# Hybrid decoder layer with mixture of experts: router logits from rows ahead of the layer norm, and second biases moved between weight chunks

## The reference

```python
xp = layer_norm(DN_ALPHA * xp + mix, ln1_g, ln1_b)
# moe_ffn
logits = (xf @ w_router + b_router).astype(F32)
top_v, top_i = lax.top_k(logits, TOP_K)          # 4 of 32
gates = jax.nn.softmax(top_v, axis=-1)
...
h = xb @ w1[e] + b1[e]
x_glu = jnp.minimum(h[:, 0::2], 7.0)
x_lin = jnp.clip(h[:, 1::2], -7.0, 7.0)
a = x_glu * jax.nn.sigmoid(1.702 * x_glu) * (x_lin + 1.0)
y = (a @ w2[e] + b2[e]) * gate
```

## Time and profile before

| | |
|---|---|
| median of 3 runs | 1467.37 us (1466.77 to 1469.71) |
| profiled execution | 1468.95 us, its span 1467.1 us |
| PE busy | 1334.4 us (91%) |
| DVE, ACT, POOL busy | 425.5, 336.8, 310.8 us |
| read from DRAM | 446.92 MB, 320 GB/s over the span |
| mean granted clock of TensorE | 0.957 |

### The profile page before, as it was taken

One profiled execution on the slowest core, in us unless ns is written; L12 is line 12 of the kernel. 1 busy time (PEld: TensorE's weight loads), 2 busy tenths in 40 slices (PEclk: granted clock), 3 DMA queues, 4 the chain that ended last, 5 costly groups with the idle time before them and its releaser, 6 DMA issues.

```text
span 1467.1 us, 32494 instructions
## 1 busy us (share of the span) xinstructions
PE 1334.4 (91%) x12921; PEld 636.8 (43%) x12921; DVE 425.5 (29%) x1085; ACT 336.8 (23%) x797; POOL 310.8 (21%) x322
## 2 busy tenths in 40 slices
PE   7999997899999999989999987899998799999871
PEld 6478765745433343433334332443433333343320
DVE  2141556656651122211112211211212121121313
ACT  1103313610022132222213122122312222131212
POOL 5215001113522221121212111122111112211103
PEclk9999997799599999999999999999999999999996
DMA  9265115070699999999999999999999999999943
GB/s 300 63 119 96 59 58 212 1 316 30 219 353 400 406 384 412 406 408 411 406 412 403 412 406 408 412 401 403 393 413 409 410 410 406 406 396 409 412 189 125
DMA packets 102821, 465.59 MB, mean 317 GB/s; under 512 B 31474, under 2 KB 41982, under 8 KB 53504
## 3 DMA queue, kind: packets, MB, share of 16 engines
q1 hardware_dynamic: 83428, 431.48, 73.5%
q0 software_dynamic: 18256, 29.88, 8.2%
q10 hardware_dynamic: 988, 2.15, 0.4%
HBM read 446.92 MB, written 22.40 MB: 320 GB/s over the span
## 4 chain that ended last, share of the span: by engine, by line
PE 48%; DMA 14%; SPq 9%; DVE 7%; issue 2%; POOL 1%; ACT 0%; DVEq 0%; POOLq 0%; ACTq 0%
PE PS L1557 24%; PE PS L1579 15%; DMA ring<-in_w_moe_dram 13%; SPq L528 6%; PE PS L1425 4%; DVE mix L2215 2%; PE PS L1570 1%; DVE qmT L2220 1%; DVE qmT L2222 1%; PE PS L1546 1%; SPq L532 1%; DVE qmT L2219 1%; SPq L536 1%; DVE qmT L2216 1%; PE PS L1485 1%
## 5 line engine op out<-in xcount | busy, mean ns | idle before, releaser
L1557 PE MATMUL PS<-ring,mix 128*32 128x512 f32 x5376 | 603.6, 596 | 52.1 <-DMA ring<-in_w_moe_dram 45.9
L1557 PEld LDWEIGHTS PS<-ring,mix 128*32 128x32 f32 x5376 | 169.4, 110 | 445.7 <-issue 343.1
L827 POOL DMA_INDIRECT expert_rows<-mix,smalls x84 | 113.6, 1353 | 803.9 <-issue 517.3
L2215 DVE TENSOR_TENSOR mix<-PS,kn 128x512 f32<-128x512 f32 x84 | 58.1, 692 | 603.1 <-PE PS L1557 599.1
L1065 ACT ACTIVATE mix<-PS,smalls 32x256 f32<-32x256 f32 x336 | 156.9, 467 | 178.2 <-PE PS L1579 172.8
L1579 PE MATMUL PS<-ring,mix 128*32 128x256 f32 x2304 | 130.4, 383 | 0.5 <-ACT mix L1059 0.5
L1049 ACT COPY mix<-PS 128x512 f32<-128x512 f32 (+1 forms) x48 | 24.1, 535 | 424.3 <-PE PS L1546 424.3
L811 POOL DMA_INDIRECT mix<-x_rows,smalls x84 | 87.0, 1036 | 40.2 <-issue 24.7
L1579 PEld LDWEIGHTS PS<-ring,mix 128*32 128x32 f32 x2304 | 73.9, 111 | 49.8 <-issue 2.8
L1579 PE MATMUL PS<-xT,mix 128*32 128x256 f32 x1536 | 93.9, 385 | 0.0
L1579 PE MATMUL PS<-X,mix 128*32 128x256 f32 x1536 | 92.0, 380 | 0.0
(11 more groups left out here) (407 smaller groups left out, 992.4 us busy)
## 6 DMA issues: line engine op xcount, KB each, us to landing
ring<-in_w_moe_dram SPq DMA_DIRECT2D x320, 1024.0 KB, 20.5
xT<-in_w_moe_dram SPq DMA_DIRECT2D x32, 1024.0 KB, 19.9
X<-in_w_moe_dram SPq DMA_DIRECT2D x32, 1024.0 KB, 21.9
ring<-in_w_in_dram SPq DMA_DIRECT2D x9, 1024.0 KB, 19.6
ring<-sample_rows SPq DMA_DIRECT2D x8, 512.0 KB, 3.9
ring<-in_w_out_dram SPq DMA_DIRECT2D x4, 1024.0 KB, 6.9
X<-in_x_prompt_dram SPq DMA_DIRECT2D x4, 512.0 KB, 8.6
ring<-in_state_mlstm_C_dram POOLq DMA_DIRECT2D x1, 2048.0 KB, 16.1
```

Source lines behind the costliest of these rows:

```text
L827: nc.gpsimd.indirect_dma_start(out=y_dram, out_offset=bass.IndirectOffsetOnAxis(ap=lists[a][0:32, g, 1:2].bitcast(U32), axis=0), in_=ysb[g ...
L1557: ins = mm(bank(BANK0[a] + g)[32 * t:32 * t + 32, :], xgT[XBUF[a][g]][:, P * (k % 2) + 32 * (k // 2):P * (k % 2) + 32 * (k // 2) + 32], sl ...
L2215: link(V.tensor_tensor(ht, bank(BANK0[a] + g), b1b, ALU.add))
```

## The change

It touches the router block and the first expert; nothing of the loop over the experts is changed. In five parts:

1. **The last tile's router works on rows ahead of the norm.** The layer norm is linear in the row up to two numbers a row, so logits = rstd * (z @ (g * W) - mean * sum(g * W)) + sum(b * W) + bias. `router_columns` makes g * W and b * W and their sums over each partition's rows once, on DVE behind the small tile's norm; `router_terms` sums them over the partitions with one matmul, and `router_constants` copies the result. Two more transfers bring g and b in columns (`ln_cols`, by single elements). For i = NT, `turn_raw` transposes the rows z in two halves, each as soon as its residual is there, ACT copies them to `rawT`, and `raw_logits` multiplies by g * W. `choose(NT)` has one more DVE operation. `normalise(NT)` stands behind `choose(NT - 1)`, and writes its first pass to `centred`, since z must stay until `turn_raw` has read it.
2. **Biases out of the chain.** Of the second biases only those of tiles 0 and 1 (first half) stand ahead of expert 0's list; their second half stands behind it, tile 2's ahead of the transposes of the gathered rows, and those of the small tile and of tile 3 between chunks of expert 0's first product.
3. On DVE, `first_ranks` of the last two tiles and the list come ahead of places, gates and all settling.
4. On POOL, `norm_power(NT)` stands behind the lists of tile 1, and the lists of tile 2 behind the gather.
5. On SP the bias row b1 of expert 1 is asked for behind all eight W1 chunks of expert 1 and W2[1][3], not behind k = 1. On ACT the lists of experts 0 and 1 are asked for ahead of the last two stores, and the activations of expert 0's first two groups on DVE come ahead of `read_list(2, ...)`.

The diff, cut to its core:

```diff
                 if i == NT - 1:
+                    act.wait_ge(raw_ready, 3)
+                    for half in range(2):
+                        act.wait_ge(x1_mm, NT + 1 + half)
+                        nc.scalar.copy(rawT[:, 4 * half:4 * half + 4, :], bank(half).rearrange("p (k n) -> p k n", n=P)).then_inc(raw_ready, 1)
                     gates_turned(0)
...
             def turn_x1(i):
-                if 0 < i < NT:
+                if i:
+            def turn_raw(half):
+                pe.wait_ge(raw_ready, 2 + half)
+                for k in range(4 * half, 4 * half + 4):
+                    ins = tr(bank(half)[:, P * (k % 4):P * (k % 4) + P], X[:, TILES[NT], P * k:P * k + P], ident)
+                ins.then_inc(x1_mm, 1)
+            def raw_logits():
+                pe.wait_ge(lg_done, NT)
+                for k in range(KT):
+                    if k % 4 == 0:
+                        pe.wait_ge(raw_ready, 4 + k // 4)
+                    ins = mm(bank(6)[:, 0:E], rawT[:, k, :], wr_gain[:, k, :], start=(k == 0), stop=(k == KT - 1))
+                ins.then_inc(lg_mm, 1)
+            def router_terms():
+                mm(bank(7)[:, 256:256 + 2 * E], ones, router_sums, start=True, stop=True).then_inc(count_mm, 1)
...
                 turn_x1(i - 1)
+                if i == NT:
+                    turn_raw(0)
                 project(i, 1, range(KT // 2, KT))
                 logits(i - 1)
-            pe.wait_ge(ln_stat, NT + 1)
+            turn_raw(1)
             turn_gates(0)
+            raw_logits()
             for i in range(NT - 1):
                 first_list(i)
+            rank_tokens(NT - 1)
+            pe.wait_ge(ln_stat, NT + 1)
             second_biases(0, 2, 0)
             second_biases(1, 3, 0).then_inc(b2_mm, 1)
-            turn_x1(NT)
-            rank_tokens(NT - 1)
-            logits(NT)
-            turn_gates(1)
-            second_biases(0, 0, 1)
-            second_biases(1, 1, 1).then_inc(b2_mm, 1)
             first_list(NT - 1)
             rank_tokens(NT)
-            second_biases(2, 2, 0)
-            second_biases(2, 3, 1).then_inc(b2_mm, 1)
-            first_list(NT)
-            pe.wait_ge(y_ready, 2)
-            second_biases(NT, 0, 0)
-            second_biases(NT, 1, 1).then_inc(b2_mm, 1)
-            turn_gates(2)
+            first_list(NT)
             mm(bank(6)[0:E, 0:E], ones[:, 0:E], SUM[:, NT, :], start=True, stop=True)
             mm(bank(6)[0:E, E:E + 1], SUM[:, NT, :], ones[:, 0:1], start=True, stop=True).then_inc(count_mm, 1)
+            second_biases(0, 0, 1)
+            second_biases(1, 4, 1).then_inc(b2_mm, 1)
+            turn_gates(1)
...
+            pe.wait_ge(gt_cp, 3)
+            pe.wait_ge(y_ready, 2)
+            second_biases(2, 3, 0)
+            second_biases(2, 4, 1).then_inc(b2_mm, 1)
             turn_tokens(0, 0, [16] * GROUPS[0])
-            second_biases(3, 3, 0)
-            second_biases(3, 4, 1).then_inc(b2_mm, 1)
             first_product(0, 0, W1[0], landed_w1(0, 0))
+            turn_gates(2)
+            first_product(0, 1, W1[1], landed_w1(0, 1))
+            pe.wait_ge(y_ready, 3)
+            second_biases(NT, 3, 0)
+            second_biases(NT, 4, 1).then_inc(b2_mm, 1)
             pe.wait_ge(order_hot, 1)
             mm(bank(5)[0:1, 0:E], tokid[0:E, 0:1], hot, start=True, stop=True).then_inc(order_mm, 1)
             mm(bank(5)[0:1, E:2 * E], rankc, ident[0:E, 0:E], start=True, stop=True).then_inc(order_mm, 1)
-            for k in range(1, 5):
+            for k in range(2, 4):
                 first_product(0, k, W1[k], landed_w1(0, k))
+            pe.wait_ge(y_ready, 4)
+            second_biases(3, 3, 0)
+            second_biases(3, 4, 1).then_inc(b2_mm, 1)
+            first_product(0, 4, W1[4], landed_w1(0, 4))
...
                 link(V.tensor_scalar(nbias[0:r], bag[0:r, 0:1], -1.0, None, ALU.mult))
-                link(V.scalar_tensor_tensor(z, z, nbias[0:r], lng[0:r, :], ALU.add, ALU.mult))
+                c = centred if i == NT else z
+                link(V.scalar_tensor_tensor(c, z, nbias[0:r], lng[0:r, :], ALU.add, ALU.mult))
                 dve.wait_ge(ln_pow, i + 1)
+                if i == NT:
+                    dve.wait_ge(x1_mm, NT + 2)
...
+            def router_columns():
+                dve.wait_ge(router_in, 64)
+                for w, v in ((0, wr_gain), (1, wr_shift)):
+                    link(V.tensor_tensor(v, wr, ln_cols[:, w, :].unsqueeze(2).to_broadcast([P, KT, E]), ALU.mult))
+                    link(V.tensor_reduce(router_sums[:, E * w:E * w + E], v.rearrange("p k e -> p e k"), AX, ALU.add), raw_ready if w else None)
...
-                if k == 1:
-                    sp.wait_ge(b1_shuf, 1)
-                    load_bias(1)
                 if k == 4:
                     sp.wait_ge(y_set, 16 * (NT - 1))
                     load_chunk(1, 11, W2[1][3])
+            sp.wait_ge(b1_shuf, 1)
+            load_bias(1)
```

133 lines of the change are left out of this document (78 added, 55 removed).

## The result

The changed kernel takes **1473.1 us** (median of 19 runs, 1466.59 to 1479.23) where the kernel before takes 1466.77 us (19 runs, 1458.63 to 1474.55). The ratio is **1.0041, interval 1.0024 to 1.0057**: slower by 0.4%, 6 us. The prediction had 1465.5 us, a range that ends at 1469.3, and a chance of 0.10 for slower by over 0.2%.

What follows compares the result with a forecast made beforehand. Weights' arrival bounds the experts, but PE's pass through expert 0 decides when their stream runs for good. Profiled 1468.95 - 2.1 + 0.2 = 1467.05; the runs' median lies 1.6 below the profiled one: 1465.5 us, range 1462.3 to 1469.3.

Steps and rivals of the forecast that it cites:

- Part 1: Router block, last tile's logits from rows ahead of the norm: experts known at 379.5 instead of 384.44, gain 4.9 us.
- Parts 2 and 3: List of expert 0 written at 382.9 instead of 390.88; first product at 395.6, 5.9 us earlier.
- What expert 0 carries: Two bias pairs between first-product chunks cost PE 3.8 us, so PE passes expert 0 2.1 us earlier.
- Clock back early: Rival: TensorE's clock is back up when the gathered rows' transposes start, 2.6 us more gained, 1463.0 us; chance 0.08.
- the skill's rule: Trainium skill: sustained activity releases TensorE's throttle; by it, tile 2's bias pair alone would bring the clock back.
- the clock stays down: Rival: TensorE stays at 1.2 GHz through expert 0's chunks k = 0 to 4 and both bias pairs, 1479 us; chance 0.09.
- The stream counts, not PE: Rival: weights set the pace from expert 1's first request, which moves 6 us, all kept, 1461.5 us; chance 0.15.
- The rest: Added DVE operations, small transfers and new queue orders: 0.2 us on the path, no more than 0.4.
- 422: Time in us from which a later W2[1][3] request on SP would cost one for one; before that, nothing.

Runs made afterwards that it cites:

- after_again: The changed kernel unaltered, run again for a second trace; ratio to the kernel before 1.0006.
- best: Changed kernel, ten DVE constant fills moved to POOL, lists of experts 0 and 1 requested before tile 2's store, expert 1's read behind first activations; ratio to before 0.9978.

## Why the prediction was wrong

Its sum up to the last chunk of expert 0 held. Point by point, with rows of the changed kernel moved by the 10.13 us between the two ends of attention (300.28 - 290.15):

```profile
379.36 3.75 PE L1519 MATMUL PS<-kva,kaT 32*128 32x512 f32 x4 [3.27 <-DVE X L2176]
...
385.10 4.34 PE L1587 MATMUL PS<-ring,mix 128*32 128x512 f32 x27 [0.52 <-ACT mix L1063]
...
391.73 1.98 PE L1519 MATMUL PS<-kva,kaT 32*128 32x512 f32 x4
```
```profile
367.45 0.25 DVE L2086 SCALAR_TENSOR_TENSOR vaug<-xT,smalls,PS 128x32 f32<-128x32 f32 x1
...
369.67 0.19 DVE L2096 TENSOR_TENSOR vaug<-vaug 128x32 f32<-128x32 f32 x1
...
373.18 0.17 DVE L2183 TENSOR_TENSOR smalls<-PS,smalls 128x6 int32<-128x6 f32 x1 [0.69 <-PE PS L1502]
```

- *Part 1.* DVE takes the last tile's logits at 377.6 (predicted 377), and the experts are known at 380.0 (379.5). The norm is what the choice waits for, as said.
- *Parts 2 and 3.* The list is written at 383.5 (382.9); PE idles 3.27 us ahead of tile 2's pair (3); the pair is at the low clock, 3.75 us. First product 395.2 (395.6): 6.3 us earlier, predicted 5.9.
- *What expert 0 carries.* First product to last chunk 23.9 us against 20.0: 3.9, predicted 3.8; the pair at the high clock 1.98, predicted 1.75. Last chunk 2.4 earlier, predicted 2.1.
- *Clock back early*, the rival with the skill's rule: it did not come. The clock was at 0.50 through the whole pair and still at 0.61 over the first 3 us of the first product. The rival *the clock stays down* did not come either: the chunks behind the first and both pairs between them ran at 1.00. The low clock behind 409 us is the effect of the wait, not a cause.
- *The stream counts, not PE*: refuted. Expert 1 to expert 5 take 36.0, 24.6, 42.6, 24.4 and 33.4 us in all kernels, PE's own pace; what is gained at expert 1 is kept, and a first request 6.6 us earlier (`after_again`) adds nothing to it.

**The step that failed is the paragraph "The rest".** It cost at nothing, or did not name, two things. First, the lists of experts 0 and 1: part 5 of the change names them, and the prediction follows the bias row and W2[1][3] past their queues, but not these two transfers. It should have asked who waits for them (DVE, idle for 6.65 us ahead of the first activations) and beside what they move: a gain that comes from letting the stream start 6 us earlier puts the stream's 8-KB packets ahead of every small transfer that stood just in front of it. The prediction asked just that of W2[1][3], and let a store land after 6.8 us; the lists needed the same sentence. W2[1][3] itself was asked for 1.2 us later than before by the run's measure in `after_again` (+117.7, before +116.5), within what was costed, and 5.6 us later in the first trace (+122.1), just past the point, 422, from which the prediction let it cost; no run prices it alone. Second, the added instructions on DVE were priced by their durations alone, and the loop 500 us later paid 1.7 to 4.0 us for their number. Nothing in the trace of before points to it: there the branch costs 0.3 us.

The losses against the forecast, in the first trace: 6.7 us at expert 1 (2.1 earlier forecast, 4.6 later measured), 1.8 us in the stream, and 1.8 us in the tail that no run explains. The first of them is that large only where the signal was late: in `after_again` expert 1 comes 2.0 us earlier than before, as forecast, and the gain is gone by 420 MB through the second alone. With the first two mended the trace of `best` is 1.8 us ahead of before at the end; the forecast had 1.9.

The rival that ended on the slower side was the wrong one, the clock. A chance of 0.10 for slower came from one mechanism, and every new order of transfers deserved one of its own.

## What to carry to other kernels

When a change lets a large stream of transfers start earlier, list every small transfer that used to be asked for just ahead of the stream, and ask what now waits behind it: here 12 KB of lists took 17.7 us from request to landing instead of 6.7. Let the small ones be asked for first, or read them behind the work that doesn't need them. Compare two traces of one kernel from the last point that the change can't have touched, not from the start, and look at the loop's branches when a program that has a loop grows, even at its start.
